# Normalising one step's probabilities between two halves of the next step's maxima

## The reference, cut to what matters

```python
s = jnp.einsum('bqhd,bkhd->bhqk', qb, kf) + bias      # scores
s = jnp.where(causal, s, -jnp.inf)
pr = jax.nn.softmax(s, axis=-1)                        # max, exp, sum, divide
# differential heads: w = pr[:, :, 0] - lam * pr[:, :, 1]
out = jnp.einsum('bhqk,bkhd->bqhd', pr, vf)            # values
```

## Time and profile before

| | |
|---|---|
| median of three runs | 3489.1 us |
| profiled execution | 3486.97 us |
| its span, first to last instruction | 3485.2 us |
| mean granted TensorE clock | 0.927 of full |
| TensorE busy | 3009.5 us (86%) |
| VectorE busy | 1122.2 us (32%) |
| ScalarE busy | 362.5 us (10%) |
| first attention | about 230 to 332 us |
| second attention | about 2345 to 2549 us |

### The profile page before, as it was taken

How to read it: one execution, slowest core, us unless ns; L and a number is a source line. 1 busy time by engine, 2 the same in 40 slices (tenths; PEclk the granted TensorE clock), 3 DMA queues, 4 the chain that set the end, 5 groups by cost and what they waited for, 6 DMA issues and landing times.

```text
span 3485.2 us, 27931 instructions
## 1 busy us (share of the span) xinstructions
PE 3009.5 (86%) x10168; PEld 1599.2 (46%) x10168; DVE 1122.2 (32%) x2244; ACT 362.5 (10%) x833; POOL 208.7 (6%) x249
## 2 busy tenths in 40 slices
PE   6998799999899688999989977667799948888885
PEld 3444344444354233444433643234444436676763
DVE  4145334200332522131032068655610032222224
ACT  1014100000110410000011000005510010000000
POOL 1000000000000000000001123400000010000000
PEclk9989999999989789999999888778999969999997
DMA  3210156421212131222223210010022129999993
GB/s 101 78 43 19 48 166 188 134 79 51 81 49 66 31 81 55 78 75 76 60 73 87 79 43 15 18 36 1 1 54 75 48 73 292 305 309 308 307 308 133
DMA packets 517755, 359.33 MB, mean 103 GB/s; under 512 B 24795, under 2 KB 479404, under 8 KB 517676
## 3 DMA queue, kind: packets, MB, share of 16 engines
q1 hardware_dynamic: 498108, 280.63, 28.0%
q0 software_dynamic: 12992, 53.53, 4.8%
q10 hardware_dynamic: 6576, 24.12, 1.8%
HBM read 328.85 MB, written 26.24 MB: 102 GB/s over the span
## 4 chain that ended last, share of the span: by engine, by line
PE 79%; DVE 11%; ACT 4%; issue 4%; DMA 1%; POOL 0%; SPq 0%; DVEq 0%; POOLq 0%; ACTq 0%
PE bank L1209 61%; PE bank L576 4%; ACT work L1433 3%; PE bank L1220 3%; PE bank L1301 2%; PE bank L480 1%; PE bank L1253 1%; PE bank L442 1%; DVE rinv L1608 1%; PE bank L470 1%; PE bank L1227 1%; DVE big L1021 1%; DVE xnT L1615 1%; PE bank L1283 1%; DVE big L1631 1%
## 5 line engine op out<-in xcount | busy, mean ns | idle before, releaser
L1209 PE MATMUL bank<-big,ring 128*128 128x128 f32 (+1 forms) x4288 | 1058.4, 408 | 96.6 <-DVE big L1021 46.6
L1209 PE MATMUL bank<-xnT,ring 128*128 128x512 f32 (+2 forms) x2400 | 1048.8, 599 | 36.8 <-DVE xnT L1615 30.2
L1209 PEld LDWEIGHTS bank<-big,ring 128*128 128x128 f32 x4288 | 622.5, 193 | 531.1 <-issue 484.6
L1209 PEld LDWEIGHTS bank<-xnT,ring 128*128 128x128 f32 (+2 forms) x2400 | 457.8, 191 | 625.0 <-issue 620.0
L1433 ACT ACTIVATE work<-bank 128x512 f32<-128x512 f32 (+2 forms) x205 | 91.3, 465 | 714.6 <-PE bank L1209 705.5
L576 PE MATMUL bank<-ring,big 128*128 128x512 f32 x320 | 146.9, 602 | 19.6 <-issue 12.9
L1874 DVE TENSOR_SCALAR work<-bank 128x512 f32<-128x512 f32 x64 | 44.3, 692 | 300.7 <-PE bank L1209 300.7
L1886 DVE COPY big<-bank 128x512 f32 x16 | 11.1, 692 | 399.4 <-ACT xnT L1433 399.3
L1227 PE MATMUL bank<-ident,big 128*128 128x128 f32 x528 | 81.3, 308 | 66.2 <-DVE big L1038 21.5
L1433 ACT ACTIVATE work<-work,nmax 128x512 f32<-128x512 f32 (+1 forms) x192 | 105.4, 552 | 317.8 <-DVE nmax L1681 317.4
L1283 PE MATMUL bank<-ident,work 128*128 128x128 f32 x440 | 71.1, 304 | 58.1 <-ACT work L1433 49.1
(11 more groups left out here) (294 smaller groups left out, 2071.9 us busy)
## 6 DMA issues: line engine op xcount, KB each, us to landing
ring<-in_moe_w_gate_dram SPq DMA_DIRECT2D x80, 512.0 KB, 5.2
ring<-in_moe_w_up_dram SPq DMA_DIRECT2D x80, 512.0 KB, 6.2
ring<-in_moe_w_down_dram SPq DMA_DIRECT2D x80, 512.0 KB, 5.4
ring<-in_mlp_w_up_dram SPq DMA_DIRECT2D x64, 512.0 KB, 4.1
ring<-in_mlp_w_down_dram SPq DMA_DIRECT2D x64, 512.0 KB, 3.8
work<-in_ada_w_dram POOLq DMA_DIRECT2D x32, 768.0 KB, 4.6
expert_out_scratch<-big ACTq DMA_DIRECT2D x42, 512.0 KB, 5.1
ring<-in_w_in_dram SPq DMA_DIRECT2D x40, 512.0 KB, 3.8
```

Source lines behind the costliest of these rows:

```text
L1209: ins = pe.matmul(bank[0:m, 0:n], w[:, q, :], rhs(k), start=(k == 0), stop=(k == total - 1))
```

## The change

Two things move in VectorE's list. Normalising step s-1 is done in iteration s instead of at the end of iteration s-1, after the first four maxima of step s and before the other four. The output copy of s-3 now comes ahead of the last probability copy of s-1. The other engines' lists, the semaphores and the buffers are the same.

```diff
@@ -1722,14 +1722,17 @@
                 for s in range(first, last + 3):
                     if s < last:
-                        for j, (h, qi) in enumerate(ORDER):
+                        for j, (h, qi) in enumerate(ORDER[0:4]):
                             largest(s, j, h, qi)
                     if first < s <= last:
-                        copy(s - 1)
+                        normalise(s - 1)
+                    if s < last:
+                        for j, (h, qi) in enumerate(ORDER[4:8]):
+                            largest(s, 4 + j, h, qi)
                     if s >= first + 3:
                         output(s - 3)
-                    if s < last:
-                        normalise(s)
+                    if first < s <= last:
+                        copy(s - 1)
```

## The result

The changed kernel takes 3533.07 us (median of four runs, 3530.58 to 3536.39) against 3488.94 for the kernel before: ratio 1.0128, 95% interval 1.011 to 1.0145. It is 44 us slower; 26 were forecast (3515, range 3497 to 3540), and the direction was right.

The account below looks back on a forecast made before the run. A chain of waits was taken as the bound: scores, first maxima, ScalarE without a pause, fifth turn, values, scores. First attention +16 and second +10 gave +26 on 3489.1 us: 3515, range 3497 to 3540.

Parts of the forecast that it names:

- The bound: Second attention: a chain of waits, not one engine, sets the period of 11.6 and 12.4 us.
- What goes: Normalising no longer ahead of the next maxima: worth 0.07 us per step without the compressed branch, 0 with it.
- What comes: Second attention: first turn starts at 3.68 instead of 0.76 us, ScalarE pauses 1.3, steps become 12.0 and 12.9.
- The chain's sum: Loss at full clock in both stretches: +11 us in the first attention, +4 in the second.
- The clock in the second attention: Second attention: about half of the steps at 0.9 us for falls on turns, +6; bounds +0 and +20.8.
- The clock in the masked steps: Masked steps 5 to 7: +1.6 us each, no clock term; step 4: +6.1, of which 1 for the clock.
- the bound of +24: First attention: upper bound of its forecast loss of +16 us, the lower being +11 at full clock.
- The clock falls in every step: Rival for both attentions: more idle time ahead of the turns, +49 us, 3538; chance 0.19 for every step or most.
- the change pays: Rival: ScalarE's exponentials cover the first turn, start gains (4.6 + 4.1) and the 0.07s remain, 3480 us; chance 0.05.
- they cancel: Rival: six clock falls vanish (second attention +4), first attention loses only 3, within 7 us of 3489; chance 0.07.

Follow-up runs that it names:

- filled kernel: The changed kernel with matmuls whose results nobody reads added in TensorE's idle time ahead of the first turn: 3495.67 us, ratio 1.0025.
- run with early values: The changed kernel with TensorE's values of step s-2 moved ahead of the first turn of s-1: 3470.29 us, ratio 0.9951.
- early values with the old order: The kernel before, normalising still at the iteration's end, with only TensorE's values moved ahead of the first turn: 3495.19 us, ratio 1.0024.
- the split after six: The changed kernel with normalising after six maxima instead of four, TensorE's idle time filled with unread matmuls: 3511.62 us, ratio 1.007.

## Why the prediction was right, and where it was not

The direction and the chain were right by their mechanism. The size was not: 3533 lies above the 3500 to 3526 that were given 0.62, and inside the range only through the room left for the clock.

- **The bound.** Right: the chain through ScalarE's copies, the fifth turn, the values and the next scores. The filled kernel repeats the worked-out periods to 0.04 us.
- **What goes.** Right that taking normalising from in front of the maxima is worth next to nothing alone: VectorE then waits for scores. In the run with early values it is worth a lot (9.76 and 10.14 us a step against 10.8 and 11.4 at best with the old order).
- **What comes.** Right: the pause was 1.21 us in the step shown, 1.3 forecast, and TensorE waited 2.94 us for the multiplies, 2.8 forecast.
- **The chain's sum.** Without clock terms I had 11 + 4 = 15 us. The filled kernel is 8.5 + 0.8 = 9.2 us longer in the two stretches (rounded after adding). The steps were right; the starts gained more than I drew at half clock (first maximum of step 2 at 13.1 us after step 0's, 15.5 forecast; of step 10 at 13.7 after step 8's, 15.2 forecast). These 9.2 us are counted against a kernel with falls of its own; the kernel before was not run filled, so what the new order costs with the clock held on both sides stays open.
- **The clock in the second attention** was a term sized too small: "about half of the steps at 0.9", +6. The price of a fall was right, their number was not: 11 of the 13 steps 10 to 22 were 0.2 to 1.9 us over the clean period, 0.9 on average and 10 us together. The fill took back 11.4 us in the whole stretch. In step 12, shown above, the fall came on turns, as drawn.
- **The clock in the masked steps** was the term that was missing. The prediction gave those steps +1.6 each for the idle time and nothing for the clock; in the kernel before they ran at 1.00. Steps 5 and 6 took 3.9 and 5.2 us more than before, and 1.5 and 1.8 more with the fill. Step 4 took 20.2 us instead of the 17.2 forecast, and 16.25 with the fill. Steps 1 to 3 came as forecast (11.38, 13.24 and 13.87 us against 11.3 and twice 13.5), so the 13 us by which the first attention was underestimated (29.3 against 16) lie in the masked steps, 4 to 7. The 29.3 also lie above the bound of +24. With the slowest period of 15.6 us in steps 2 and 3 the terms shown give only +20, and steps 5 to 7 have no clock term in either sum.
- **The page on the clock.** The Trainium skill, page "TensorE: Matmul & The Clock Gate", section "HAM oscillation — how this bites in real kernels", tells of a kernel in which each tile's compute is shorter than the wait for data behind it, and the clock is throttled again in every single tile. That is not this case: TensorE worked longer than it waited here (1.55 us idle in masked steps of 18.57 and 19.78 us). The clock fell all the same, in masked steps 4 to 7 and in 11 of those 13 steps of the second attention (0.87 on average there).
- **The rivals.** "The clock falls in every step" (3538) came nearer than my forecast in mechanism and size (3533 was measured, 3515 forecast); "the change pays" was measured only with the values moved too; "they cancel" is out.
- **Open:** in which steps of the second attention a fall comes, and why early values with the old order draw more of them than the kernel before; the falls were seen and priced, their order was not explained. Of the orders tried, only the changed one and the split after six were run filled.

## What to carry to other kernels

Before an operation is moved later on one engine, ask who is in line for its result on the others: here ScalarE's copies stood ahead of exponentials that were ready, so the delay went through the whole loop. An idle microsecond given to TensorE can cost more than itself where the clock falls behind it: here 1.55 us of it made two masked steps, which TensorE bounds, 3.9 and 5.2 us longer, against 1.5 and 1.8 with the clock held. A run with the idle time filled by unread matmuls separates the two costs. A reorder that opens a wait can be half of a good one if other work on that engine can be moved into the wait, as the values were here.

## What the runs showed of the hardware

- 1.55 us of idle TensorE ahead of the transposes of step 6 were followed by 9.1 us at the half level (clock 0.50). The same stage ran at 1.00 in the kernel before, with 0.77 us of idle time in steps 5 and 6.
- Matmuls into a bank that is overwritten anyway, in that idle time, kept the clock at 0.98 and 0.99 (0.76 and 0.87 without) and took the kernel from 3533 to 3496 us, though TensorE had some 140 more matmul instructions. Transposes run at the full rate then: eight in 1.09 us, against 1.94.
